# Start bytes in SBUF of the seven-product slabs: all their weights at byte 192 of 256, all their moving operands at byte 0

## The chip, the core and the metric

The kernel runs on one core of a Trainium2 chip. The metric is the device time of one execution in microseconds (us); the median of several executions stands for a kernel. A profile of one further execution gives each instruction's start on each engine. The two levels of TensorE's clock are 1.2 and 2.4 GHz; the profile gives the granted share of the full one. Throughout, "byte 192" is a start address in an SBUF partition modulo 256 bytes (64 float32 words, the constant `LINE`).

## What is computed

A forward pass over 512 tokens of width 1024, in float32: two gated feed-forward layers (width 2816) around a mixing layer with dilated attention and multi-scale pooling, then a retention layer and a stick-breaking attention layer. Cut to what the change touches:

```
def swiglu(x, w1, w3, w2):
    return (jax.nn.silu(x @ w1) * (x @ w3)) @ w2

h = h + 0.5 * swiglu(rms_norm(h, ffn1_norm[l]), ffn1_w1[l], ffn1_w3[l], ffn1_w2[l])
u = rms_norm(h, mix_norm[l])
proj = u @ w_in[l]                 # q, k, v, pooled part, two gates
...
merged = gates[:, :, 0] * y_attn + gates[:, :, 1] * y_pool
h = h + merged @ w_out[l]
h = h + 0.5 * swiglu(rms_norm(h, ffn2_norm[l]), ffn2_w1[l], ffn2_w3[l], ffn2_w2[l])
...
proj = u @ ret_w_in[i]             # q, k, v, g of the retention layer
```

## The kernel before

**Numbers.** Each float32 operand is split in a high and a low part (`w_hi` and `w_lo`, `x_hi` and `x_lo`), and a product is three matmuls: high weights by high x, high weights by low x, low weights by high x. These are the lines 2570 to 2572 (`passes`) and 2576 to 2578 (`joint`). In the trace's names the moving operand or the weights may come second: `acc<-x_hi,w_lo` has x moving and the low weights stationary, `acc<-w_hi,x_hi` has the slab moving and x stationary (value projections).

**Slabs.** Weights come in slabs of 2048 words a partition into `raw` (two slots, `RING`), by DMAs of the SP queue. ScalarE writes the high part (L736 for a plain slab), VectorE the low part (L1454), and TensorE works through them. TensorE may start on a slab when `w_ready` counts it; SP fetches the next into a slot when `w_ready` says that `raw` has been read. A plain slab is used in matmuls with 512 moving columns.

**Seven-product slabs.** Where a slab yields two independent 512x128 outputs from the same x, seven products of half size replace eight (Strassen's scheme). The program calls this `seven`. Each of the seven is 4 chunks of 3 matmuls, so 12 matmuls of 128x128 weights by 256 moving columns, 84 a slab. There are 57 such slabs in 8 stretches that follow on a plain slab: 7 and 11 in the first feed-forward layer, 2, 2 and 2 in the mixing layer, 8 and 11 in the second feed-forward layer, 14 in the retention layer (with four small transposes after the fourth of them, L2631). Four quarters of weights lie in the slab's slot (`s2`, `a11`, `s1`, `s3`), three in `wc_hi` and `wc_lo` (`a12`, `a22`, `s4`). The moving operands are quarters of `x_hi`/`x_lo` or the combinations `t1`, `t2`, `t3` in `xt_hi`/`xt_lo`.

The start bytes follow from the sizes of the tensors that are allocated ahead: `w_hi`, `w_lo`, `x_hi`, `x_lo` and `t4` start at byte 0, `xt_hi`, `xt_lo`, `wc_hi` and `wc_lo` at byte 192. A weight block is 512 bytes, a chunk of x 1024 or 2048, so all 12 matmuls of a product have the same two start bytes:

| product, in TensorE's order | weights | byte of weights, before | byte of moving operand, before | both after |
|---|---|---|---|---|
| 1 | a11 in w | 192 | 0 (x) | 192, 0 |
| 2 | s3 in w | 0 | 192 (t3 in xt) | 192, 0 |
| 3 | s2 in w | 0 | 192 (t2 in xt) | 192, 0 |
| 4 | a12 in wc | 192 | 0 (x) | 192, 0 |
| 5 | s1 in w | 0 | 192 (t1 in xt) | 192, 0 |
| 6 | a22 in wc | 192 | 0 (x or t4) | 192, 0 |
| 7 | s4 in wc | 192 | 0 (x) | 192, 0 |

Between products stand semaphore waits: ScalarE copies partial results out of PSUM (`snap`, L835; `snap_ready`) before products 3, 5 and 7 add to the same bank, and products 4 and 7 wait for the weights in `wc` (`wc_ready`). The order on every engine is written out by hand. ScalarE makes the slab's high parts in L780 (two quarters, `split_pair`) and L785 (the other two, `split_one`, which writes through the view `lone`), VectorE the low parts in L1556 and L1561. Ahead of the change `lone` spans two pieces, one at byte 0 and one at 192.

`first_col(k)` gives the column at which slab number k starts in its slot: 48 words (byte 192) for slabs of value projections, 0 for all others. Both the splitting (`prep`) and TensorE's `slab` use it, and `w_hi` and `w_lo` have 64 spare words a slot for it.

## Time and profile before

| | us |
|---|---|
| median of 3 executions | 1847.12 (1846.47 to 1848.96) |
| the profiled execution | 1845.56 |
| its span, first to last instruction | 1843.8 |
| TensorE busy in the span | 1828.2 (99%) |
| TensorE weight loads busy | 1636.9 (89%) |
| VectorE, ScalarE, GpSimd busy | 1396.5, 930.0, 81.5 |
| granted TensorE clock | 0.998 of full |

The profiled execution is 1.8 us from start to end longer than its span; what is taken off the span comes off it alike. It lies 1.6 us under the median. Matmuls overlap in the array and their ends are modelled, so what TensorE spends on a matmul is read from the distance of its start to the next start, and not from its duration.

### The profile page before, as it was taken

The page shows a single profiled execution, that of the slowest core. Times are in us where ns is not written, and L with a number is a line of the kernel's source. Part 1 is how long each engine was busy: PE and PEld are TensorE (multiplying, and loading weights), DVE is VectorE, ACT ScalarE, POOL GpSimd, SP SyncE. Part 2 cuts the span into 40 slices and gives each one's busy share as a digit, 9 for nine tenths or more (in the row PEclk, how much of TensorE's full clock was granted, in tenths as well). Part 3 has the DMA queues.
Part 4 walks back from the last instruction along what each step waited for, and adds up shares of the span by engine and source line. Part 5 has one row for each costly group of instructions (what it writes and reads, how often), then busy time and mean ns, then how long its engine had stood idle before and what let it go on. Part 6 is the DMA issues. An engine that isn't in the chain of part 4 may idle for free.

```text
span 1843.8 us, 28142 instructions
## 1 busy us (share of the span) xinstructions
PE 1828.2 (99%) x11305; PEld 1636.9 (89%) x11311; DVE 1396.5 (76%) x1912; ACT 930.0 (50%) x1274; POOL 81.5 (4%) x109
## 2 busy tenths in 40 slices
PE   9999999999999999999999999999999999999997
PEld 7998998888889988988998899988888888888886
DVE  8875887888778889866888987776777776666566
ACT  6652664435355536633653555455547644444445
POOL 0000000020001000000000000000000000000000
PEclk9999999999999999999999999999999999999999
DMA  6744763462407535743752678632231222222213
GB/s 215 181 120 133 199 161 116 164 158 77 114 26 210 155 114 149 188 149 110 191 146 95 199 211 240 231 137 77 107 137 61 79 92 69 92 81 79 91 68 92
DMA packets 60595, 244.78 MB, mean 133 GB/s; under 512 B 6865, under 2 KB 9457, under 8 KB 49857
## 3 DMA queue, kind: packets, MB, share of 16 engines
q1 hardware_dynamic: 46016, 199.25, 32.3%
q0 software_dynamic: 14032, 43.38, 12.3%
q8 instruction: 80, 1.31, 0.3%
q10 hardware_dynamic: 432, 0.56, 0.1%
q14 instruction: 35, 0.28, 0.0%
HBM read 223.76 MB, written 13.11 MB: 128 GB/s over the span
## 4 chain that ended last, share of the span: by engine, by line
PE 72%; DVE 5%; ACT 2%; issue 1%; DMA 0%; DVEq 0%; POOL 0%; ACTq 0%
PE acc L2570 14%; PE acc L2571 13%; PE acc L2572 13%; PE acc L2577 6%; PE acc L2576 6%; PE acc L2578 6%; PE att L2571 2%; PE att L2572 2%; PE att L2570 2%; PE att L2576 1%; PE att L2578 1%; PE att L2577 1%; DVE w_lo L1454 1%; PE acc L2838 1%; PE acc L2813 1%
## 5 line engine op out<-in xcount | busy, mean ns | idle before, releaser
L1454 DVE TENSOR_TENSOR w_lo<-raw,w_hi 128x2048 fp32r<-128x2048 f32 (+1 forms) x106 | 238.9, 2254 | 48.7 <-ACT w_hi L736 48.4
L736 ACT ACTIVATE w_hi<-raw 128x2048 fp32r<-128x2048 f32 (+1 forms) x106 | 199.3, 1880 | 75.3 <-PE acc L2572 61.9
L2570 PE MATMUL acc<-x_hi,w_hi 128*128 128x512 f32 x488 | 193.3, 396 | 0.9 <-DVE x_lo L1517 0.6
L2576 PE MATMUL acc<-xt_hi,w_hi 128*128 128x256 f32 x684 | 191.6, 280 | 0.0
L2578 PE MATMUL acc<-xt_hi,w_lo 128*128 128x256 f32 x684 | 191.3, 280 | 0.0
L2577 PE MATMUL acc<-xt_lo,w_hi 128*128 128x256 f32 x684 | 191.3, 280 | 0.0
L2572 PE MATMUL acc<-x_hi,w_lo 128*128 128x512 f32 x488 | 190.3, 390 | 0.0
L2571 PE MATMUL acc<-x_lo,w_hi 128*128 128x512 f32 x488 | 190.1, 390 | 0.0
L835 ACT ACTIVATE tmp<-acc 128x256 f32<-128x256 f32 x228 | 86.8, 380 | 124.6 <-PE acc L2578 114.8
L2571 PE MATMUL acc<-g_lo,w_hi 128*128 128x512 f32 x352 | 137.0, 389 | 0.0
L2570 PE MATMUL acc<-g_hi,w_hi 128*128 128x512 f32 x352 | 137.0, 389 | 0.0
L2572 PE MATMUL acc<-g_hi,w_lo 128*128 128x512 f32 x352 | 136.9, 389 | 0.0
L2576 PEld LDWEIGHTS acc<-xt_hi,w_hi 128*128 128x128 f32 x684 | 130.1, 190 | 0.1
L2578 PEld LDWEIGHTS acc<-xt_hi,w_lo 128*128 128x128 f32 x684 | 128.4, 188 | 0.0
L2577 PEld LDWEIGHTS acc<-xt_lo,w_hi 128*128 128x128 f32 x684 | 128.4, 188 | 0.0
L2570 PEld LDWEIGHTS acc<-x_hi,w_hi 128*128 128x128 f32 x488 | 91.6, 188 | 23.0 <-issue 2.7
L2576 PE MATMUL acc<-x_hi,wc_hi 128*128 128x256 f32 x400 | 110.5, 276 | 0.0
L2578 PE MATMUL acc<-x_hi,wc_lo 128*128 128x256 f32 x400 | 110.4, 276 | 0.0
L2577 PE MATMUL acc<-x_lo,wc_hi 128*128 128x256 f32 x400 | 110.4, 276 | 0.0
L2571 PEld LDWEIGHTS acc<-x_lo,w_hi 128*128 128x128 f32 x488 | 91.7, 188 | 20.1 <-issue 1.4
L2572 PEld LDWEIGHTS acc<-x_hi,w_lo 128*128 128x128 f32 x488 | 91.6, 188 | 19.2
L792 ACT ACTIVATE wc_hi<-raw_c 128x1024 fp32r<-128x1024 f32 x57 | 60.4, 1059 | 50.8 <-PE acc L2578 50.8
(510 smaller groups left out, 5116.0 us busy)
## 6 DMA issues: line engine op xcount, KB each, us to landing
raw<-in_ffn_down SPq DMA_DIRECT2D x32, 704.0 KB, 4.0
raw_c<-in_ffn_seven SPq DMA_DIRECT2D x37, 512.0 KB, 5.3
raw<-in_ffn_seven SPq DMA_DIRECT2D x33, 512.0 KB, 4.9
raw<-in_ffn_seven POOLq DMA_DIRECT2D x33, 512.0 KB, 7.4
raw<-in_ffn_seven SPq DMA_DIRECT2D x37, 256.0 KB, 4.6
raw<-in_ret_values SPq DMA_DIRECT2D x8, 1024.0 KB, 4.7
raw<-in_ret_out SPq DMA_DIRECT2D x8, 1024.0 KB, 6.8
raw<-in_sb_v SPq DMA_DIRECT2D x8, 1024.0 KB, 4.8
```

The costliest lines, as they stand in the source:

```text
L736: nc.scalar.activation(w_hi[:, slot, at:at + cols], raw[:, slot, 0:cols], ACT.Copy).then_inc(w_hi_ready, 1)
L792: nc.scalar.activation(wc_hi[:, cols], raw_c[:, third, :], ACT.Copy).then_inc(wc_hi_ready, 1)
L835: nc.scalar.activation(dst, src, ACT.Copy).then_inc(snap_ready, 1)
L1454: tt(w_lo[:, slot, at:at + cols], raw[:, slot, 0:cols], w_hi[:, slot, at:at + cols].bitcast(F32), ALU.subtract).then_inc(w_ready, 1)
L2570: mm(dst, still[0], move[0], start=first, stop=False)
L2571: mm(dst, still[0], move[1], start=False, stop=False)
L2572: return mm(dst, still[1], move[0], start=False, stop=last)
L2576: mm(dst, still[0], move[0], start=first, stop=False, skip_group_check=True)
L2577: mm(dst, still[0], move[1], start=False, stop=False, skip_group_check=True)
L2578: return mm(dst, still[1], move[0], start=False, stop=last, skip_group_check=True)
L2813: last = nc.tensor.transpose(dst[i // TB][:, P * (i % TB):P * (i % TB) + P], tmp[:, at:at + P], ident[:])
L2838: last = mm(dst, va[:, k_blk, value_slot(g, head)].rearrange("p s d -> p (s d)"), turned_probs[:, k % 2, i].rearrange("p s q -> p (s q)"), ...
```

## The change

No instruction is added, removed or put elsewhere: each engine has the same list in the same order. What differs is where operands lie.

- In a seven-product slab the four quarters lie one behind the other from byte 192 of the slot (`LATER_LINE`, 48 words). Before, they stood at words 0, 560, 1088 and 1600 of the slot: bytes 0, 192, 0 and 0. `lone` becomes one contiguous piece, `W_SUMMED` starts 16 words earlier.
- `xt_hi` and `xt_lo` move from byte 192 to byte 0, by padding ahead of them that is 48 words less, and 48 words more behind. `wc`, `x`, `t4` and all else stay.
- The plain slab ahead of each of the 8 stretches (`BEFORE_SEVEN`) starts at byte 192 instead of 0. These are 8 slabs with 318 matmuls of 512 columns in all: three of 48 (`x` by the last plain slab of the two feed-forward layers and the retention layer), two of 33 (the last down-projection slab of each first half) and three of 36 (the branch slabs of the mixing layer). Their moving operands are at byte 0.

```
--- before.py
+++ after.py
@@ -38,11 +38,12 @@
 MIX_SEVEN = DC - MIX_PLAIN
 QUART = SLAB // PARTS
 SUMMED = slice(2 * QUART, SLAB)
-W_SUMMED = slice(2 * QUART + 64, SLAB + 64)
 FILLED = {4: 2, 5: 2, 6: 1, 7: 2}
 PART = SLAB // PARTS
 RING = 2
 LINE = 64
+LATER_LINE = LINE * 3 // 4
+W_SUMMED = slice(LATER_LINE + 2 * QUART, LATER_LINE + SLAB)
 MIX_VALUES = 43, 44, 49
 SB_FIRST = 136
 BANKS = 4
@@ -196,7 +197,7 @@
 
         def lone(v, slot):
 
-            return v[:, slot, 0:2 * (QUART + LINE * 3 // 4)].rearrange("p (k q) -> p k q", k=2)[:, :, 0:QUART]
+            return v[:, slot, LATER_LINE:LATER_LINE + 2 * QUART].rearrange("p (k q) -> p k q", k=2)
 
         def pair_place(slot, ahead):
 
@@ -210,7 +211,7 @@
         def first_col(k):
 
             values = k in MIX_VALUES or k >= SB_FIRST and (k - SB_FIRST) % 4 == 0
-            return LINE * 3 // 4 if values else 0
+            return LATER_LINE if values or k in BEFORE_SEVEN else 0
 
         def half_row(c):
             return slice(TOK // 2 * (c % 2), TOK // 2 * (c % 2 + 1))
@@ -232,10 +233,10 @@
                 form_q = sb("form_q", [P, TB, TOK // 2], F32, under)
                 form_b = sb("form_b", [P, TB, TOK // 2], F32, under)
             g_lo = sb("g_lo", [P, HALF, TOK], F32R, scope)
-            sb("to_line_4", [P, 48 + 3 * DC * P], F32, scope)
+            sb("to_line_4", [P, 3 * DC * P], F32, scope)
             xt_hi = sb("xt_hi", [P, 3, TB, TOK // 2], F32R, scope)
             xt_lo = sb("xt_lo", [P, 3, TB, TOK // 2], F32R, scope)
-            sb("to_line_5", [P, 16], F32, scope)
+            sb("to_line_5", [P, LINE], F32, scope)
             raw_c = sb("raw_c", [P, RING, 2 * QUART], F32, scope)
             sb("to_line_6", [P, 48], F32, scope)
             wc_hi = sb("wc_hi", [P, 3 * QUART], F32R, scope)
@@ -453,6 +454,9 @@
         RET_FROM = sum(FFN_SEGS) + MIX_SEGS
         HEADS_FROM = RET_FROM + 2 * RET_PLAIN + PRODUCTS * RET_SEVEN
         UNIT_SLABS_FROM = 2 * (FC + 2 * DC) + MIX_SLABS
+        FFN_SLABS_FROM = 0, FC + 2 * DC + MIX_SLABS
+        BEFORE_SEVEN = ([FFN_SLABS_FROM[i] + FULL[i] - 1 for i in range(2)] + [FFN_SLABS_FROM[i] + HALF + DC - 1 for i in range(2)] +
+                        [FC + 2 * DC + BRANCH_FROM + 3 * j for j in range(1, DC // 2)] + [UNIT_SLABS_FROM + RET_PLAIN - 1])
         ACC_BEFORE_RET = 206
 
         def head_end(i, part):
@@ -2661,7 +2665,7 @@
                 slot = n.k % RING
                 n.next()
                 s2, a11, s1, s3 = ((w_hi[:, slot, at:at + QUART], w_lo[:, slot, at:at + QUART]) for at in
-                                   (0, QUART + LINE * 3 // 4, 2 * QUART + LINE, 3 * QUART + LINE))
+                                   (LATER_LINE + QUART * k for k in range(PARTS)))
                 a12, a22, s4 = ((wc_hi[:, QUART * k:QUART * (k + 1)], wc_lo[:, QUART * k:QUART * (k + 1)]) for k in range(3))
                 b11, b21, b22 = ((x_hi[:, rows, cols], x_lo[:, rows, cols]) for rows, cols in
                                  ((slice(0, TB), EARLY), (slice(TB, DC), EARLY), (slice(TB, DC), LATE)))
```

## Rows read from the trace of the kernel before

**Rows 1.** The page: busy time by engine, granted clock in 40 slices, chain by engine.

```profile
PE 1828.2 (99%) x11305; PEld 1636.9 (89%) x11311; DVE 1396.5 (76%) x1912; ACT 930.0 (50%) x1274; POOL 81.5 (4%) x109
...
PEclk9999999999999999999999999999999999999999
...
PE 72%; DVE 5%; ACT 2%; issue 1%; DMA 0%; DVEq 0%; POOL 0%; ACTq 0%
```

**Rows 2.** Timeline of TensorE, one seven-product slab: start us, modelled us, line, names.

```profile
219.89 0.28 PE L2576 MATMUL acc<-x_hi,w_hi 128*128 128x256 f32 x1
...
221.25 0.28 PE L2576 MATMUL acc<-xt_hi,w_hi 128*128 128x256 f32 x1
...
222.67 0.28 PE L2576 MATMUL acc<-xt_hi,w_hi 128*128 128x256 f32 x1
...
224.08 0.28 PE L2576 MATMUL att<-x_hi,wc_hi 128*128 128x256 f32 x1
...
225.50 0.28 PE L2576 MATMUL acc<-xt_hi,w_hi 128*128 128x256 f32 x1
...
226.87 0.28 PE L2576 MATMUL acc<-x_hi,wc_hi 128*128 128x256 f32 x1
...
228.23 0.28 PE L2576 MATMUL acc<-x_hi,wc_hi 128*128 128x256 f32 x1
...
229.59 0.28 PE L2576 MATMUL acc<-x_hi,w_hi 128*128 128x256 f32 x1
```

**Rows 3.** Line 2576 by names: count, modelled ns min/median/max, first and last start.

```profile
L2576 PE MATMUL acc<-xt_hi,w_hi x684: 276/281/387, 54.6 to 1183.8; 128*128 128x256 f32 x171
...
L2576 PE MATMUL att<-x_hi,wc_hi x228: 276/280/283, 57.5 to 1182.4; 128*128 128x256 f32 x114
```

**Rows 4.** Timeline of TensorE, first slab of a stretch: starts of products 1 and 2.

```profile
570.90 0.28 PE L2576 MATMUL acc<-x_hi,w_hi 128*128 128x256 f32 x1
...
572.31 0.28 PE L2576 MATMUL acc<-xt_hi,w_hi 128*128 128x256 f32 x1
```

**Rows 5.** Timeline of TensorE, last seven-product slab: products 3, 4, 5 and the end.

```profile
1179.71 0.28 PE L2578 MATMUL acc<-xt_hi,w_lo 128*128 128x256 f32 x1
1179.87 0.39 PE L2576 MATMUL acc<-xt_hi,w_hi 128*128 128x256 f32 x1
...
1181.35 0.28 PE L2576 MATMUL att<-x_hi,wc_hi 128*128 128x256 f32 x1
...
1182.71 0.28 PE L2576 MATMUL acc<-xt_hi,w_hi 128*128 128x256 f32 x1
...
1186.96 0.40 PE L2570 MATMUL acc<-w_hi,x_hi 128*128 128x512 f32 x1
```

**Rows 6.** Timeline of TensorE, the slab behind the four transposes of the retention stretch.

```profile
1089.31 0.60 PE L2631 MATMUL att<-ident,rstd 128*128 128x128 f32 x4
...
1089.98 0.28 PE L2578 MATMUL acc<-x_hi,w_lo 128*128 128x256 f32 x1
...
1091.11 0.28 PE L2576 MATMUL acc<-xt_hi,w_hi 128*128 128x256 f32 x1
```

**Rows 7.** Timeline of TensorE, value projection: first and last of 48 matmuls.

```profile
429.83 0.28 PE L2570 MATMUL acc<-w_hi,x_hi 128*128 128x256 f32 x1
...
435.37 0.28 PE L2572 MATMUL acc<-w_hi,x_lo 128*128 128x256 f32 x1
```

**Rows 8.** Timeline of TensorE, 264 matmuls of 512 columns between two stretches.

```profile
121.18 0.40 PE L2570 MATMUL acc<-g_hi,w_hi 128*128 128x512 f32 x1
...
181.04 0.28 PE L2576 MATMUL acc<-x_hi,w_hi 128*128 128x256 f32 x1
```

**Rows 9.** Windows: PE, PEld, DVE, ACT, POOL busy (count), clock, DMA share, GB/s.

```profile
210.20:219.90 9.70, 9.70 (x87) 9.70 (x86) 8.36 (x13) 6.17 (x10) 0.86 (x1) 1.00 0.74 196
```

**Rows 10.** Timeline of ScalarE in the slab of rows 2: the first snap.

```profile
221.45 0.38 ACT L835 ACTIVATE tmp<-acc 128x256 f32<-128x256 f32 x1
```

**Rows 11.** Lines by form: the split through `lone` on ScalarE, busy us, mean ns.

```profile
L785 ACT ACTIVATE w_hi<-raw 128x1024 fp32r<-128x1024 f32 x57 | 60.1, 1054 | 4.9 <-DVE raw L1543 4.9
```

More of the change, by code:

```diff
@@ L40 @@
 SUMMED = slice(2 * QUART, SLAB)
-W_SUMMED = slice(2 * QUART + 64, SLAB + 64)
 FILLED = {4: 2, 5: 2, 6: 1, 7: 2}
@@ L45 @@
 LINE = 64
+LATER_LINE = LINE * 3 // 4
+W_SUMMED = slice(LATER_LINE + 2 * QUART, LATER_LINE + SLAB)
 MIX_VALUES = 43, 44, 49
@@ L197, in lone @@
         def lone(v, slot):
-            return v[:, slot, 0:2 * (QUART + LINE * 3 // 4)].rearrange("p (k q) -> p k q", k=2)[:, :, 0:QUART]
+            return v[:, slot, LATER_LINE:LATER_LINE + 2 * QUART].rearrange("p (k q) -> p k q", k=2)
         def pair_place(slot, ahead):
@@ L212, in first_col @@
             values = k in MIX_VALUES or k >= SB_FIRST and (k - SB_FIRST) % 4 == 0
-            return LINE * 3 // 4 if values else 0
+            return LATER_LINE if values or k in BEFORE_SEVEN else 0
         def half_row(c):
@@ L234, in block_kernel @@
             g_lo = sb("g_lo", [P, HALF, TOK], F32R, scope)
-            sb("to_line_4", [P, 48 + 3 * DC * P], F32, scope)
+            sb("to_line_4", [P, 3 * DC * P], F32, scope)
             xt_hi = sb("xt_hi", [P, 3, TB, TOK // 2], F32R, scope)
             xt_lo = sb("xt_lo", [P, 3, TB, TOK // 2], F32R, scope)
-            sb("to_line_5", [P, 16], F32, scope)
+            sb("to_line_5", [P, LINE], F32, scope)
             raw_c = sb("raw_c", [P, RING, 2 * QUART], F32, scope)
@@ L455, in block_kernel @@
         UNIT_SLABS_FROM = 2 * (FC + 2 * DC) + MIX_SLABS
+        FFN_SLABS_FROM = 0, FC + 2 * DC + MIX_SLABS
+        BEFORE_SEVEN = ([FFN_SLABS_FROM[i] + FULL[i] - 1 for i in range(2)] + [FFN_SLABS_FROM[i] + HALF + DC - 1 for i in range(2)] +
+                        [FC + 2 * DC + BRANCH_FROM + 3 * j for j in range(1, DC // 2)] + [UNIT_SLABS_FROM + RET_PLAIN - 1])
         ACC_BEFORE_RET = 206
@@ L2663, in seven @@
                 s2, a11, s1, s3 = ((w_hi[:, slot, at:at + QUART], w_lo[:, slot, at:at + QUART]) for at in
-                                   (0, QUART + LINE * 3 // 4, 2 * QUART + LINE, 3 * QUART + LINE))
+                                   (LATER_LINE + QUART * k for k in range(PARTS)))
                 a12, a22, s4 = ((wc_hi[:, QUART * k:QUART * (k + 1)], wc_lo[:, QUART * k:QUART * (k + 1)]) for k in range(3))
```

## The prediction

> **What bounds the kernel now.** The page comes first. TensorE is busy 99% of the span at the full clock (2.4 GHz), and 72% of the chain that ended last is its own work, against 5% for VectorE and 2% for ScalarE [rows 1]. So time is won or lost where matmuls follow each other faster or slower, and a change of addresses can act there alone, unless another engine comes on top. The second view is the timeline of TensorE in one seven-product slab [rows 2]. Each product is 12 matmuls, so the distance of two starts over 12 is the pace of one matmul. Products 1, 6 and 7 take 1.36 us (113.3 ns a matmul), product 5 takes 1.37, products 2, 3 and 4 take 1.42, 1.41 and 1.42 (118 ns). The slab takes 9.70 us. The reader is to see two paces, 113.3 and about 117.9 ns, of instructions of one shape.
>
> The third view groups line 2576 by names [rows 3]. The modelled durations show the same two paces: the 684 matmuls with `xt` moving (products 2, 3 and 5) have a median of 281 ns and a minimum of 276, and product 4, whose operands lie at the same bytes as those of products 6 and 7, has 280 and 276. **The pair of start bytes alone does not set the pace.** Product 4 (192, 0) is slow and 6 and 7 (192, 0) are fast; products 2 and 3 (0, 192) are slow and 5 (0, 192) is fast. The pace behaves as a state that the stream carries along. I went through the boundaries of the 57 slabs for where it turns:
> - From (192, 0) to (0, 192), as from product 1 to 2 and 4 to 5, it turns: fast to slow, then slow to fast [rows 2].
> - From (0, 192) to (192, 0), as from 3 to 4 and 5 to 6, it stays what it was [rows 2].
> - Where the bytes stay the same (2 to 3, 6 to 7, and 7 to the next slab's 1) it stays too. In the last slab a stall of 0.16 us ahead of product 3 (1179.71 to 1179.87, 0.05 more than a step) turned the slow stream fast. Product 4 then took 1.36 us, and products 5 to 7 ran slow (4.25 us for 36 matmuls, 118 ns), over the boundary of 6 and 7 with its semaphore waits [rows 5]. So waits that are met early do not turn it, and a slow stream goes on at equal bytes.
> - Behind the plain slab, whose weights and x are both at byte 0, product 1 is slow: 1.41 us instead of 1.36, in 8 of 8 stretches [rows 4]. Behind the transposes it is fast (10 matmuls in 1.13 us) [rows 6].
>
> **The change part by part.** The order of all instructions stays, so each part is a price per matmul.
>
> *Seven-product slabs.* All 84 matmuls get (192, 0), the pair of the fast products 6, 7 and 1. No boundary within a stretch changes bytes any more. If the stream is fast, a slab takes 84 x 113.3 ns = 9.52 us instead of 9.70: 0.18 us less. 57 slabs give 10.3 us.
>
> *The entry.* 8 first slabs lose a slow product 1, 12 x 4.6 ns = 0.05 us each, 0.4 us. The last slab has 36 slow matmuls where others have none, and some fewer elsewhere; it gives about 0.05 us more. Sum: 10.7 us. Both the stall there and the one behind the transposes stay.
>
> *Whether the entry is fast.* This decides the sign, and the trace has no stream of 512 columns at (192, 0). Now the entry is a jump from (0, 0) to (192, 0), with 8 of 8 slow. With the plain slab at byte 192 as well there is no jump, only the change from 512 to 256 columns. All the turns in the steady slabs stand at boundaries where bytes change, so I take the entry as fast. But the rows do not exclude that the full 512-column stream ahead is itself what starts the slow pace: the value projection behind the pooling matmuls also starts slow out of 512-column matmuls, and keeps 117.9 ns for 47 steps (429.83 to 435.37) [rows 7].
>
> *The 8 plain slabs.* Their 318 matmuls of 512 columns run at 226.7 ns now: 264 of them take 59.86 us [rows 8]. At (192, 0) they could at worst pay the 4.6 ns that the slow 256-column matmul pays: 318 x 4.6 = 1.5 us. The start bytes have no visible price in the long streams, and a few steps where they change are under 0.03 us a slab. I take 0, nearest to rows 8, and keep 1.5 for the range; nothing below 0, since the mean there is exactly two fast steps of 256.
>
> *Other engines.* A seven-product slab costs VectorE 8.36 and ScalarE 6.17 of its 9.70 us [rows 9]. At 9.52 they still fit, with 1.1 us left on VectorE. The tightest wait is that on `snap`: it starts at 221.45, lasts 0.38, and TensorE wants it for product 3 at 222.67, 0.84 us later [rows 2, 10]. Product 2, which covers it, gets only 0.06 us shorter. If the cover were gone, each stall would be paid in full, as the one in rows 5. `lone` in one piece is the same 1024 words, 1054 ns on ScalarE [rows 11]; it is off TensorE's path, cost 0. The DMA share of 0.74 rises to about 0.75. All this goes at nothing.
>
> Against the profiled execution: 1845.56 - 10.7 = 1834.9 us, and since what changes is inside the span, the median goes from 1847.12 to **1836.4 us**, 0.58% less.
>
> **The rivals.**
> - *Slow throughout.* If 512 columns into 256 starts slow whatever the bytes, nothing turns the stream back before its end: today the turn from product 4 to 5 does that in every slab, and the change removes it. A slow slab takes 84 x 117.9 = 9.90 us, 0.20 more than now. That holds for the 47 slabs ahead of the transposes and elsewhere; the 10 behind them start fast [rows 6] and gain 0.18. 47 x 0.20 - 10 x 0.18 = +7.6 us: 1854.7 us. It decides in the first matmuls of each stretch; for it speak rows 7 and the persistence in rows 5, against it that every turn in steady slabs comes with a change of bytes. If the 10 also fell slow, it were +11.4 us, 1858.5.
> - *Some stretches.* Entries could differ: the mixing layer's come out of branch slabs with `o_hi` moving, others out of `x` or `g`. Or a slow entry heals after some slabs. Half the slabs fast and half slow is about zero, three quarters fast gives -10.3 x 0.75 + 57 x 0.25 x 0.20 = -4.9 us. So 1839 to 1847, centre 1842. For it: the entries are 8 separate events. Against it: all 8 are alike now.
> - *It does nothing.* The pace may come from what is read against what in time, not from start bytes, with the turns made by something else that stands at the same products; then 1847.1 us. For it: one pair of bytes has both paces [rows 2]. Against it: the turns repeat in each slab at the same boundaries. The Trainium skill is on this rival's side: the page "SBUF — State Buffer", section "Who interferes with whom", says that TensorE has two independent read ports, one for the moving operand and one for the weights, and waits on nobody. By that rule no address would matter, and the trace does not agree as far as the pace goes: equal shapes at 113.3 and 118 ns.
>
> **How the numbers follow.** Fast throughout: 0.58, at 1836.4 us, of its own range 1835 to 1838.5 (the 1.5 us of the plain slabs, and 0.5 either way for the executions). Some stretches: 0.12. Nothing: 0.10. Slow: 0.20. The predicted time is that of the first. The range must leave out no more than 0.2: it runs from 1834.5 to 1850.0, over the first three cases and up to what a partly slow kernel gives, and leaves out the slow one. A measurement of this kernel tells about 0.2% (3.7 us) from no change, so faster is below 1843.4 and slower above 1850.8. Faster takes the 0.58 and 0.09 of the mixed case, 0.67; same takes 0.03 of that and the 0.10, 0.13; slower 0.20.
>
> **What would show it.** In the changed kernel's timeline the starts of all seven products of a slab should be 1.36 us apart and a slab 9.52; the group with `xt` moving should have a median of 276 ns like the others, and the group into `att` too. Product 1 of a stretch's first slab shows the entry: 1.36 us for fast, 1.41 for slow, and in the latter case the whole stretch should show 1.41 until its end, except behind the transposes. The plain slabs at byte 192 should keep 227 ns. Snap ends should lie over 0.7 us ahead of product 3, and VectorE's sum in a slab should stay near 8.4 us. The prediction is wrong if entries are slow, if fast streams turn slow at equal bytes, or if the 512-column matmuls at (192, 0) run slower.

## The result

The changed kernel took **1856.99 us** (median of 5 runs, 1855.19 to 1857.53) where the kernel before, run beside it, took 1846.74 (5 runs, 1846.34 to 1848.96): a ratio of 1.0053, with an interval of 1.0042 to 1.0065. It is 0.53% slower. The prediction had been 1836.4 us with a range up to 1850.0, so sign and range are both wrong. The time is nearest to that of the rival "slow throughout" in its harder form, 1858.5 us, in which the ten slabs behind the transposes are slow too; it lies 1.5 us below it.

The page of the changed kernel (span 1855.2 us, 1843.8 before) shows where the time is. First the busy time by engine and the clock, then the chain by engine:

```profile
PE 1840.1 (99%) x11305; PEld 1648.6 (89%) x11311; DVE 1396.8 (75%) x1912; ACT 931.8 (50%) x1274; POOL 81.5 (4%) x109
...
PEclk9999999999999999999999999999999999999999
...
PE 94%; DVE 3%; ACT 1%; issue 1%; DMA 0%; DVEq 0%; ACTq 0%; POOL 0%
```

Against [rows 1] the counts of instructions are the same and the clock is the same. VectorE and ScalarE grew by 0.3 and 1.8 us, TensorE by 11.9, and the chain went from 72% TensorE to 94%. So the added time is TensorE's own. Where it is, the timeline shows for the slab that answers to [rows 2]. The columns are start, modelled us, line and names; the lines of the changed kernel are four higher:

```profile
212.26 0.28 PE L2580 MATMUL acc<-x_hi,w_hi 128*128 128x256 f32 x1
...
213.67 0.28 PE L2580 MATMUL acc<-xt_hi,w_hi 128*128 128x256 f32 x1
...
216.50 0.28 PE L2580 MATMUL att<-x_hi,wc_hi 128*128 128x256 f32 x1
217.91 0.28 PE L2580 MATMUL acc<-xt_hi,w_hi 128*128 128x256 f32 x1
219.33 0.28 PE L2580 MATMUL acc<-x_hi,wc_hi 128*128 128x256 f32 x1
...
222.15 0.28 PE L2580 MATMUL acc<-x_hi,w_hi 128*128 128x256 f32 x1
```

Product 1 takes 1.41 us (213.67 - 212.26), products 2 and 3 together 2.83, product 4 1.41, product 5 1.42, products 6 and 7 together 2.82. The slab takes 9.89 us: 84 matmuls at 117.8 ns. The two paces inside a slab are gone, as forecast, but what is left is the slow one.

Two groups of the view by names answer to [rows 3] (count, modelled ns min/median/max, first and last start):

```profile
L2580 PE MATMUL acc<-xt_hi,w_hi x684: 279/279/279, 54.8 to 1195.2; 128*128 128x256 f32 x171
...
L2580 PE MATMUL att<-x_hi,wc_hi x228: 279/279/279, 57.6 to 1193.8; 128*128 128x256 f32 x114
```

Minimum, median and maximum are one number. Before, the minimum was 276, the mark of the fast pace. All 57 slabs run slow from the first to the last, without one exception. They take 564.00 us in sum, 553.65 before: **10.35 of the 11.4 us**. The rest is in two places. The 318 matmuls of 512 columns in the plain slabs now follow each other at 226, 229 and 232 ns in turn, 228.8 on average instead of 226.7 [rows 8], which is 0.7 us. And 96 matmuls of 256 columns of the value projection at 410.9 us, which the diff does not touch, run at 117.8 ns instead of 113.3, 0.4 us. (In both traces that projection begins behind a stall of 0.14 to 0.16 us, out of which it came fast in the one and slow in the other.)

### The profile page after: what moved, and what is told of

Read it like the earlier page. It is cut to its first block, busy times and chain, and to the rows that moved or that the text cites. A ratio compares the mean times of both kernels' runs of the same rounds, so it can differ in the third digit from the quotient of the medians.

```text
span 1855.2 us, 28142 instructions
## 1 busy us (share of the span) xinstructions
PE 1840.1 (99%) x11305; PEld 1648.6 (89%) x11311; DVE 1396.8 (75%) x1912; ACT 931.8 (50%) x1274; POOL 81.5 (4%) x109
## 4 chain that ended last, share of the span: by engine, by line
PE 94%; DVE 3%; ACT 1%; issue 1%; DMA 0%; DVEq 0%; ACTq 0%; POOL 0%
PE acc L2574 17%; PE acc L2575 17%; PE acc L2576 17%; PE acc L2582 9%; PE acc L2581 9%; PE acc L2580 9%; PE att L2575 2%; PE att L2576 2%; PE att L2574 2%; PE att L2582 1%; PE att L2581 1%; PE att L2580 1%; PE acc L2842 1%; PE acc L2817 1%; DVE w_lo L1458 0%
```

## The experiments

A pair like (192, 0) is the start byte of the weights and of the moving columns. "Slow" and "fast" are the paces of 117.8 and 113.3 ns a matmul of 256 columns, 9.893 and 9.520 us a slab. The 512-column matmuls of a plain slab have their own, longer steps. A step is the distance of one matmul's start to the next start; "entered behind a 226" says that the step from the last 512-column matmul to the first 256-column one of a stretch was 226 ns. Most kernels below were run once, and are judged by the steps and slabs in their trace and not by their time; where a ratio with an interval stands, there were several runs. Two theories stand against each other at the start: that the entry from the plain slabs starts the slow pace and nothing turns it back, and that the bytes themselves have a price.

**Each half alone.** The first kernel takes only the plain slabs back, the second is the kernel before with only the plain slabs moved.

```
 # e1_sevens_only, against the changed kernel
-            return LATER_LINE if values or k in BEFORE_SEVEN else 0
+            return LATER_LINE if values else 0
 # e2_plain_only, against the kernel before
-            return LINE * 3 // 4 if values else 0
+            return LINE * 3 // 4 if values or k in BEFORE_SEVEN else 0
```

> The change without its last part: the plain slab ahead of each stretch stays at byte 0, the seven-product slabs are all at (192, 0). Theory H (the pace is carried along: the stretch keeps the pace with which it is entered, and out of 512-column matmuls that pace is slow): all 57 slabs slow at 9.89 us as in the changed kernel, the 318 matmuls of the plain slabs back at 226.7 ns instead of 228.8, so about 1856.3 us, 0.7 under the changed kernel. Rival P (the plain slab at byte 192 is what makes the entry slow): product 1 fast at 1.36 us and slabs of 9.52 us, about 1836 us.

> The kernel before with the plain slab ahead of each stretch at byte 192 and nothing else. Theory H: product 1 of each stretch stays slow at 1.41 us, the later slabs stay at 9.70 us with products 2, 3 and 4 slow, and the 318 matmuls of 512 columns cost 2.1 ns more each, 0.7 us: 1847.8 us. Rival P: product 1 takes another pace than 1.41 us, and products 5 to 7 may turn slow, over 1850 us.

Sevens only: 1856.17 us against 1846.63, ratio 1.0050 (1.0033 to 1.0066), all 57 slabs slow. Plain slabs only: 1847.75 against 1846.63, ratio 1.0003 (0.9994 to 1.0013), slabs of 9.70 us as before. The loss is that of the sevens. The plain slabs' new byte, which was to make the entry fast, made it fast in two of eight stretches: the second and third mixing stretch of this kernel begin with a product 1 of 1.36 us (first slab 9.700 us, 9.748 in the other unstalled ones), against theory H's "stays slow". The other six were entered behind a 226, these two behind a 232. In the kernel with only the sevens changed all eight are slow, behind a 225 or 226. The difference of the two kinds of entry comes back below.

**Other bytes for the weights.** `SEVEN_AT` stands in the place of 48 words in the sevens and in the plain slabs ahead of them: 16 words (byte 64), then 32 (byte 128).

```
+SEVEN_AT = 16
+W_SUMMED = slice(SEVEN_AT + 2 * QUART, SEVEN_AT + SLAB)
...
+            return LATER_LINE if values else SEVEN_AT if k in BEFORE_SEVEN else 0
```

> The changed kernel with all seven-product weights (w and wc) and the 8 plain slabs at byte 64 instead of 192, moving operands at byte 0. Theory H (any equal pair keeps the pace of the entry): slabs of 9.89 us, 1857 us. Rival D (each difference of start bytes has a pace of its own, and that of 192 and 0 is a slow one): another pace, at best 9.52 us a slab and 1836 us, at worst the 120 ns that matmuls at equal bytes show elsewhere, 10.1 us a slab and 1868 us.

> As with byte 64, now byte 128 for all seven-product weights and the 8 plain slabs. Theory H: slabs of 9.89 us, 1857 us. Rival D: another pace, between 9.52 us a slab (1836 us) and 10.1 us a slab (1868 us).

At byte 128 every slab takes 9.96 to 9.98 us (two with a stall more), 1862.83 us in all, and the steps wander between 112 and 125 ns instead of keeping to one pace: those bytes do have a price of their own. At byte 64 (1850.86 us, span 1849.1) something new appears. The 22 slabs of the two stretches behind the down projection run fast from their first product, the 35 of the other six are slow, at the same bytes and with the same code. So at byte 64 the bytes alone do not set the pace; it differs from stretch to stretch, by how a stretch is entered or by what it is.

**Byte 64 with other plain slabs.** Only the plain slabs' byte differs from the run at 64: `0` or `LATER_LINE` in place of `SEVEN_AT` in the last line above.

> Seven-product weights at byte 64 as in the run before, where the two stretches of 11 behind the down-projection ran fast (9.52 us a slab) and the six others slow (9.89), but the 8 plain slabs ahead stay at byte 0. Theory H (the entry decides, and the pace is then carried on at equal bytes): the entries from byte 0 make some stretches fast or slow as a whole; from (0, 0) the entry to (192, 0) was always slow, so all slow, 1856 us. Rival C (what made two entries fast is the down-projection's own count or operands, not its byte): the same two stretches stay fast, about 1848.5 us.

> Seven-product weights at byte 64, the 8 plain slabs ahead at byte 192. Theory H: each stretch is fast or slow as a whole by its entry; nothing says which, between 1836 and 1857 us. Rival C: again the two stretches of 11 fast and the others slow, about 1849 us. A pace that changes within a stretch at equal bytes speaks against H.

With plain slabs at 0 all 57 slabs are slow (1856.85 us, span 1855.1). With plain slabs at 192 (1855.21, span 1853.4) the first mixing stretch had a stall of 0.4 us ahead of product 5 and one of 0.1 us behind its first matmul, ran fast from the fifth matmul of product 5 on, and the next two mixing stretches were then entered fast, behind a 233; all others were slow, behind a 225 or 226. Rival C falls in both kernels. The pace did change within a stretch at equal bytes, which had been named as a sign against H, but it did so at a stall: a short stall can turn the pace, and the next stretch, behind a slab of 512-column matmuls, was then fast too.

**One product with other bytes.** In the changed kernel without its plain slabs' move, product 5 alone gets its old pair (0, 192), by its own place for `s1` and `t1`:

```
-                                   (LATER_LINE + QUART * k for k in range(PARTS)))
+                                   (2 * QUART + LATER_LINE, 3 * QUART + LATER_LINE, 0, QUART + LATER_LINE))
...
+XT_AT = LATER_LINE, LINE + TB_COLS, LINE + 2 * TB_COLS
...
```

> All seven products at (192, 0) but the fifth, whose weights stay at byte 0 and whose moving combination t1 stays at byte 192; plain slabs at byte 0. Theory T (the jump from (192, 0) to (0, 192) turns the pace, the way back does not): the pace turns once a slab, so slabs alternate: one with products 1 to 4 slow and 5 to 7 fast, the next with 1 to 4 fast and 5 to 7 slow, about 9.71 us on average, about 1847 us. Rival A (a uniform (192, 0) falls back to slow by itself, and fast needs a jump in each slab): products 5 to 7 fast and 1 to 4 slow in every slab or all slow, 1848 to 1856 us.

1848.86 us, span 1847.1. The timeline of two neighbouring slabs, first matmuls of their products:

```profile
196.04 0.28 PE L2594 MATMUL att<-x_hi,wc_hi 128*128 128x256 f32 x1
...
197.46 0.28 PE L2594 MATMUL acc<-xt_hi,w_hi 128*128 128x256 f32 x1
...
198.83 0.28 PE L2594 MATMUL acc<-x_hi,wc_hi 128*128 128x256 f32 x1
...
201.55 0.28 PE L2594 MATMUL acc<-x_hi,w_hi 128*128 128x256 f32 x1
...
205.63 0.28 PE L2594 MATMUL att<-x_hi,wc_hi 128*128 128x256 f32 x1
...
206.99 0.28 PE L2594 MATMUL acc<-xt_hi,w_hi 128*128 128x256 f32 x1
...
208.41 0.28 PE L2594 MATMUL acc<-x_hi,wc_hi 128*128 128x256 f32 x1
```

Product 4 takes 1.42 us (slow), product 5 1.37, products 6 and 7 2.72 together (fast). The next slab is still fast in product 4 (1.36) and slow from product 5 on (1.42). Each slab's one change to (0, 192) turns the pace and it is carried on over the slab's boundary, so that slabs alternate between 9.745 and 9.688 us. In the first slab of seven stretches the change turns nothing (9.896 us, slow throughout); in that of the first mixing stretch a stall ahead of product 5 comes on top, and it is fast behind it.

**Turning it with idle matmuls.** These kernels are built on the one with only the sevens changed (sevens at 192, plain slabs at 0, all slow). Ahead of product 4, or of products 2 and 4, of each stretch's first slab they issue idle matmuls with the pair (0, 192), whose result the product overwrites. Shown is the version with four at each of two places; in the others the number is 1 or 12, or only the second place is used:

```
+            def turn(dst, behind):
...
+                if behind in BEFORE_SEVEN:
+                    for _ in range(4):
+                        mm(dst, x_hi[:, TB + 1, 0:P], x_hi[:, TB + 1, 48:48 + TOK // 2], start=True, stop=True, skip_group_check=True)
...
+                turn(one[:, EARLY], n.k - 2)
                 product(one[:, EARLY], s3, t3, True)
...
+                turn(aside, n.k - 2)
+                product(aside, a12, b21, True)
```

> Sevens all at (192, 0), plain slabs at byte 0, and in the first slab of each stretch four idle matmuls of 256 columns ahead of product 4, with weights at byte 0 and moving operand at byte 192, whose result product 4 overwrites. Theory T (one such jump turns the pace, and equal bytes then keep it): products 1 to 3 of the first slab slow, all behind it fast, slabs of 9.52 us, about 1840 us. Rival A (a uniform (192, 0) is slow by itself): back to slow behind the four, about 1860 us.

> The sevens as in the changed kernel, the plain slabs back at byte 0 (the run with only the sevens changed: profiled span 1854.7 us, all 57 seven slabs slow, 9.893 us). In the first seven slab of each of the eight stretches, four idle matmuls with weights at byte 0 and moving columns at byte 192 stand ahead of product 2 and four more ahead of product 4; their result is overwritten by the product behind them. Theory A (the pace of a stretch is a state that equal bytes carry on; behind 512-column matmuls the first change of bytes doesn't turn it, the second does): in a first slab products 1 to 3 stay at 117.8 ns a matmul, products 4 to 7 run at 113.3, and all 49 slabs behind the first ones take 9.52 us. Slabs: 49 x 0.37 = 18.3 us less; first slabs 8 x 48 x 4.5 ns = 1.7 less, and 8 x 8 idle matmuls x 0.118 = 7.6 more: span near 1842.3, the time near 1844. Theory B (what turned the pace in the kernel before is not the change of bytes itself but something that idle matmuls lack, such as the products' own length, so they turn nothing, as four ahead of product 4 turned nothing): all slabs stay at 9.893, span 1854.7 + 7.6 = 1862.3.

> As the kernel with four idle matmuls ahead of products 2 and 4 of each first slab, but with one at each place instead of four. Theory A: if one matmul at other bytes is a change of bytes as good as four, the pace turns from product 4 on and the slabs behind take 9.52 us; cost 8 x 2 x 0.118 = 1.9 us, gain 18.3 + 1.7: span near 1836.6, the time near 1839, a ratio to the kernel before of 0.996. If the turn needs more than one matmul at the other bytes: all slow, 1854.7 + 1.9 = 1856.6. Theory B says that too: 1856.6.

> As the kernel with four idle matmuls at weights 0 and moving 192 ahead of products 2 and 4 of each first slab (all slow, 1861.9 us), with twelve at each place, as many as a product has. If a stay at other bytes must be as long as a product's to turn the pace, a first slab runs fast from product 4 on and the 49 slabs behind take 9.520 us: 1854.7 + 8 x 24 x 0.118 - 49 x 0.373 - 1.7 = 1857.4. If idle matmuls that read one place again and again don't turn it whatever their number, all stay slow: 1854.7 + 22.7 = 1877.4.

One group of four: all slow, 1860.45 us. Two groups of four: all slow, 1863.65 us, with a span of 1861.9 where the rival, that idle matmuls turn nothing, had said 1862.3. Two groups of one: all slow, 1858.31 us against 1846.12, ratio 1.0066 (1.0049 to 1.0083). After these the theory that a change of bytes turns the pace looked fallen. The last run, with twelve at each place, brought it back. The timeline of its stretch at 182.9 us, first matmuls of products and the groups of idle ones (line 2666):

```profile
182.86 0.28 PE L2580 MATMUL acc<-x_hi,w_hi 128*128 128x256 f32 x1
...
184.27 1.58 PE L2666 MATMUL acc<-x_hi 128*128 128x256 f32 x12
...
185.68 0.28 PE L2580 MATMUL acc<-xt_hi,w_hi 128*128 128x256 f32 x1
...
188.51 1.53 PE L2666 MATMUL att<-x_hi 128*128 128x256 f32 x12
...
189.88 0.28 PE L2580 MATMUL att<-x_hi,wc_hi 128*128 128x256 f32 x1
...
191.25 0.28 PE L2580 MATMUL acc<-xt_hi,w_hi 128*128 128x256 f32 x1
```

Behind the first group product 2 is slow (with product 3, 2.83 us for 24). The second group itself takes 1.37 us and what follows is fast: product 4 1.37, and the slab behind 9.520. That is so in all eight stretches. So the second change of bytes turns a slow stream when the stay at the other bytes is twelve matmuls long, and not when it is four. Of the 49 slabs behind first slabs 42 were entered fast, at the changed kernel's own bytes. The span is 1861.5 against 1857.4 expected: the last slabs of the four longer stretches ahead of the retention layer take 9.84 (1.3 us more), since a stall ahead of product 5 (steps of 167 and 224 to 228 ns) turns them slow, and a like stall between products 4 and 5 of the third slab behind the transposes (slab 49, counted from 0) turned it and the seven behind it slow (3.0 us more).

**Counting the matmuls in front.** In the run at byte 64 the 512-column matmuls of the plain slabs follow each other at 231 and 236 ns in turn. The eight entries, with the last three steps of 512 columns and the first three of 256, worked out from the starts in the trace's records, in the run at 64 and in the one with matmuls added that follows:

```
byte 64, none added                   byte 64, one added in six
 start  last 512     first 256         start  last 512     first 256
  53.3  232 236 230  119 116 119        53.9  236 231 236  118 113 114
 182.6  236 232 236  117 114 114       180.8  236 230 236  119 113 113  none added
 571.0  231 235 231  119 117 117       569.3  236 231 236  118 114 113
 599.1  231 235 231  119 117 117       597.6  233 233 234  121 116 114
 627.3  232 235 230  120 117 117       625.2  230 236 231  118 118 117
 724.6  231 237 231  117 119 117       722.7  235 231 236  118 114 113
 863.8  235 231 236  118 114 112       859.1  236 231 235  119 113 113  none added
1052.4  231 236 231  117 119 117      1048.0  236 231 236  118 114 113
```

Without one added, the two fast stretches (182.6 and 863.8) are entered behind a 236, the six slow stretches behind a 230 or 231. So the first matmul of the plain slab is issued once more, in the six slow cases, and in a second kernel in all eight:

```
+            again = set(set(BEFORE_SEVEN) - {FFN_SLABS_FROM[i] + HALF + DC - 1 for i in range(2)})
...
             def passes(dst, still, move, first, last):
...
+                if first and n.k - 1 in again:
+                    again.remove(n.k - 1)
+                    mm(dst, still[0], move[0], start=True, stop=True)
```

> Base: the kernel with the weights of sevens and of the plain slabs in front of them at byte 64 (one look: 1850.86 us, profiled span 1849.1; the 22 slabs of the two stretches behind the down projection run 9.520 us, the 35 of the six other stretches 9.893). In its plain slabs the 512-column matmuls follow each other at 231 and 236 ns in turn; the two fast stretches were entered on a 236, the six slow ones on a 230 or 231. Here the first matmul of the plain slab in front of each of the six slow stretches is issued twice (once more 128x512, overwritten by the second), and nothing else is changed. Theory P (the pace at the entry is the phase in which the stream of matmuls stands to the reads of SBUF, and the parity of the matmuls at byte 64 sets it): all eight stretches are entered on a 236 and all 57 slabs run 9.52 us; 35 x 0.373 = 13.1 us less, 6 x 0.233 = 1.4 more, span near 1837.4, the time near 1839.2, a ratio to the kernel before of 0.996. Theory Q (the pace at the entry hangs on what the stretch or its slab is, not on the count): the same two stretches are fast, span 1849.1 + 1.4 = 1850.5.

> As the kernel with one more matmul in six of the plain slabs, but with one in all eight, so also in front of the two stretches that were fast before. Theory P: the count's parity turns there too, so that these two are entered on a 231 and their 22 slabs go to 9.893 while the 35 others go to 9.520: span 1849.1 - 13.1 + 22 x 0.373 + 8 x 0.233 = 1846.1. Theory Q: as before, 22 fast and 35 slow, 1849.1 + 1.9 = 1851.0.

Here one matmul alone changes the pace. The entry of the first stretch, byte 64 without the added matmul, then with it:

```profile
52.83 0.40 PE L2576 MATMUL acc<-x_lo,w_hi 128*128 128x512 f32 x1
53.07 0.39 PE L2577 MATMUL acc<-x_hi,w_lo 128*128 128x512 f32 x1
53.30 0.28 PE L2581 MATMUL acc<-x_hi,w_hi 128*128 128x256 f32 x1
53.42 0.28 PE L2582 MATMUL acc<-x_lo,w_hi 128*128 128x256 f32 x1
53.53 0.28 PE L2583 MATMUL acc<-x_hi,w_lo 128*128 128x256 f32 x1
53.65 0.28 PE L2581 MATMUL acc<-x_hi,w_hi 128*128 128x256 f32 x1
```

```profile
53.47 0.39 PE L2581 MATMUL acc<-x_lo,w_hi 128*128 128x512 f32 x1
53.70 0.40 PE L2582 MATMUL acc<-x_hi,w_lo 128*128 128x512 f32 x1
53.94 0.28 PE L2586 MATMUL acc<-x_hi,w_hi 128*128 128x256 f32 x1
54.06 0.28 PE L2587 MATMUL acc<-x_lo,w_hi 128*128 128x256 f32 x1
54.17 0.28 PE L2588 MATMUL acc<-x_hi,w_lo 128*128 128x256 f32 x1
54.28 0.28 PE L2586 MATMUL acc<-x_hi,w_hi 128*128 128x256 f32 x1
```

The last 512-column matmul is modelled at 0.39 us and followed by a step of 0.23 in the one, and modelled at 0.40 with a step of 0.24 in the other, and the fourth start comes 0.35 and 0.34 us behind the first. That is how small the sign is; what it tells lasts for seven slabs, 9.893 us each against 9.520 (9.693 in the last, which has a stall). With one added in six, five of these six stretches and the two others are entered fast: 1843.73 us against 1846.30, ratio 0.9985 (0.9975 to 0.9994), span 1840.7. The sixth, the third mixing stretch, was slow. With one in all eight (1849.01 us, span 1847.2), the two stretches behind the down projection became slow, all 22 slabs at 9.893, and the five stretches other than the second mixing one fast. Theory Q, that the pace hangs on the stretch, falls. One entry in the table stands outside the pattern: the second mixing stretch (597.6) was fast out of even steps of 233 ns, with no long and short ones in turn. For the six a span of 1837.4 was expected and 1840.7 came, 3.3 us more. Some 2.3 us are two stretches that turned slow midway. The first of these turns comes with a stall of 0.04 us:

```profile
574.65 0.28 PE L2588 MATMUL att<-x_hi,wc_lo 128*128 128x256 f32 x1
574.76 0.32 PE L2586 MATMUL acc<-xt_hi,w_hi 128*128 128x256 f32 x1
574.91 0.28 PE L2587 MATMUL acc<-xt_lo,w_hi 128*128 128x256 f32 x1
575.03 0.28 PE L2588 MATMUL acc<-xt_hi,w_lo 128*128 128x256 f32 x1
```

The matmul that opens product 5 holds 0.04 us longer than its neighbours (0.32), the next starts 0.15 us behind it instead of 0.11, and what follows is slow to the end of the stretch. (The program has a semaphore wait ahead of this product; the view of waits lists none on TensorE here, so that the stall is a wait is taken from its place.) Slab 52 has a like stall at product 5 (0.08 us), and the four behind it are slow. The last slabs of two more stretches have a stall (0.35 us together). The rest, 0.75 us, is the third mixing stretch, slow from its entry: with a matmul added, each had the opposite pace of the one before it; without one, in the run at 64, the same.

**The same count at the change's own bytes.** In the changed kernel the steps in front go 226, 229, 232, and all eight stretches are entered behind a 226. One or two matmuls more move that:

```
+            more = {k: 2 for k in BEFORE_SEVEN}
...
             def passes(dst, still, move, first, last):
...
+                if first:
+                    for _ in range(more.pop(n.k - 1, 0)):
+                        mm(dst, still[0], move[0], start=True, stop=True)
```

> The changed kernel (weights of sevens and plain slabs at byte 192, x at 0; span 1855.2 us, all 57 seven slabs at 9.893) with the first 512-column matmul of each of the eight plain slabs issued three times instead of once, nothing else. In these slabs of the changed kernel the matmuls follow each other at 226, 229 and 232 ns in turn, and all eight stretches are entered behind a 226. With the plain slabs at 192 and the sevens at 64 two stretches were fast, both entered behind a 233. Theory P (a phase that each matmul moves on, and where the last 512-column one leaves it sets the pace of all that follows): two more move each entry on by two, to behind a 232 or 233, and all 57 slabs run 9.520 us: 57 x 0.373 = 21.3 less, 16 x 0.229 = 3.7 more, span near 1837.6. Theory Q (the cycle belongs to the operands, which come in threes, and repeating one moves nothing; the pace at these bytes is the slow one): 1855.2 + 3.7 = 1858.9.

> As the changed kernel with two more matmuls in each plain slab, but with one more. Theory P: the entries come behind a 229; whether that phase is a fast or a slow one no run has shown. The fast one is one of three here, so slow is the likelier: span 1855.2 + 8 x 0.229 = 1857.0; were it fast, 1855.2 - 21.3 + 1.8 = 1835.7. Theory Q: 1857.0, with the entries behind a 226 as in the changed kernel.

With two more, six of the eight stretches are entered behind a 231 or 232 and are fast from the first step; the second mixing one is entered behind a 229 and the third behind a 226, both slow. With one more, seven are entered behind a 229 or 230 and one behind a 226, all slow, 1859.41 us. The two kernels differ from the changed one by 16 and 8 matmuls and from each other by 8:

```
first stretch          last 512      first 256         pace
changed kernel         229 232 226   117 119 117       117.8
one more               231 226 229   120 118 117       117.8
two more               226 229 232   113 113 114       113.3
```

So the entry at (192, 0) is slow in the changed kernel because of where in the cycle it happens to fall. With two more the time was 1847.07 us, the span 1845.3 and not 1837.6. The 4 slabs of the two mixing stretches are slow (1.5 us), and so are those behind the transposes, which turned the stream here (3.4 for nine); stalls in the last two slabs cost 1.3, and the last slabs of the four longer stretches take 9.84 us (1.3).

**No cycle, no count.** With the plain slabs at byte 0 the steps are an even 226.7 ns; one matmul more in front of four stretches, two in front of the others:

```
+            more = {k: 1 + i % 2 for i, k in enumerate(sorted(BEFORE_SEVEN))}
```

> The kernel with only the sevens changed (plain slabs at byte 0, all 57 seven slabs at 9.893 us, span 1854.7) with one more 512-column matmul in front of the first, third, fifth and seventh stretch and two more in front of the others; nothing else. At byte 0 the 512-column matmuls follow each other at an even 226.7 ns, so that there is no cycle that a count could move. Theory P in its narrow form (only matmuls that go in a cycle have a phase to hand on): every stretch is entered behind a 226 and stays slow, span 1854.7 + 12 x 0.227 = 1857.4. Theory P in its wide form (a count moves the phase at any bytes): the stretches with one or those with two more turn fast, some 9 to 12 us less: 1845 to 1849.

1861.37 us, every slab slow and every entry behind a 225 or 226: there is nothing that a count could move. The span is 2.2 us above the expected 1857.4, by waits in the first mixing slab and in the last two slabs. Nine kernels here, the one before among them, have their plain slabs at byte 0, and all 72 entries are slow, as the 8 of 8 of the kernel before [rows 4]. Whether the even steps or the jump of bytes does it there is not separated, since each of the nine has both. Elsewhere the jump does not decide: the changed kernel has none and is slow, and with the plain slabs at 192 and the sevens at 64 two entries over a jump are fast.

**A version that beats both.** Byte 64, one matmul added in four plain slabs, none in front of the second and third mixing stretch:

```
...
+            more = {k: 1 for k in BEFORE_SEVEN[:2] + BEFORE_SEVEN[4:5] + BEFORE_SEVEN[-1:]}
```

> The kernel with the weights of sevens and plain slabs at byte 64 and one more matmul in six of the eight plain slabs had three slow pieces left: the slab behind a short wait in the first mixing stretch and its neighbour, the third mixing stretch, and five slabs at the end behind another short wait. Here the second and third mixing stretch get no additional matmul, since from one mixing stretch to the next a fast one without an additional matmul should stay fast; four are added in all. Theory P: all eight stretches are entered on a 236; with no wait in a stretch all 57 slabs run 9.520, span 1837.0; each wait of a stretch can turn the rest of it, at 0.37 us a slab: 1837.0 to 1840.5, the time 1838.5 to 1843. Theory Q: the two stretches without an additional matmul are slow as in the kernel with none, 1.5 us more than that.

**1842.39 us** (10 runs, 1839.23 to 1842.89) against 1846.28 (13 runs): ratio 0.9975, interval 0.9966 to 0.9985. It is 0.25% faster than the kernel before. In the profiled execution (span 1838.1) all 57 slabs are fast, 544.44 us in sum, 1.8 above 57 x 9.52 by stalls. The group with `xt` moving, to be set beside [rows 3]:

```profile
L2586 PE MATMUL acc<-xt_hi,w_hi x684: 276/276/387, 55.0 to 1178.0; 128*128 128x256 f32 x171
```

Three of its ten runs took 1839.2 to 1839.9 us, seven 1842.3 to 1842.9. One profile shows one of the first kind; that in the others a stall turned some eight slabs slow (8 x 0.37 = 3.0 us) is argued from the other traces, not shown. A stall does not turn the stream always: in this profile one at product 5 of slab 18 cost 0.46 us, and the fast pace went on behind it.

```profile
574.74 0.28 PE L2588 MATMUL att<-x_hi,wc_lo 128*128 128x256 f32 x1
575.20 0.39 PE L2586 MATMUL acc<-xt_hi,w_hi 128*128 128x256 f32 x1 [0.18 <-ACT tmp L840]
575.42 0.28 PE L2587 MATMUL acc<-xt_lo,w_hi 128*128 128x256 f32 x1
```

The last slabs of the long stretches show more of this. A fast stream meets a like stall there at product 5. With the weights at byte 64 (steps of 164 to 169 and 221 to 223 ns) it stayed fast in 12 of 12 cases, in four kernels (slab 9.69 us). With the weights at 192 (166 to 168 and 224 to 228 ns) it came out slow in 8 of 8 (9.84 us), in the kernel with two more matmuls and the one with twelve idle ones. So byte 64 holds the fast pace better over this stall. Why is not shown.

## Why the prediction was wrong

- **What bounds the kernel** was right: all of the difference is TensorE's own pace, at the same count of instructions and the same clock. That the pace is a state which the stream carries along was right too, and each later run leans on it.
- **"Whether the entry is fast"** is the step that failed. It took the entry as fast because in the steady slabs all turns stand where bytes change, and so gave 0.58 to the fast case. The trace of before had two signs against it, and the text named both: 8 of 8 entries slow [rows 4], and a slow value projection behind 512-column matmuls [rows 7]. It read the first as a jump of bytes that the change would remove. The runs show that the pace follows the last step of the 512-column stream (at unchanged bytes slow behind a 226 or 229, fast behind a 232), and that equal bytes give no claim to the fast one. A third sign was not named: the prediction says that the change from (192, 0) to (0, 192) turns the pace, but in the eight first slabs of before product 2 is slow behind a slow product 1 (both 1.41 us), so that there the change of bytes turned nothing. And the slow case lost more than the entry: in the kernel before, the change at product 5 brought each slab back to the fast pace, as the run with product 5 alone and the one with twelve idle matmuls show; the rival said this, the main case did not need it.
- **Seven-product slabs.** The sizes were right to 0.01 us: 9.52 for a fast slab, in every run that had some, and 9.893 for a slow one where the rival had 9.90. Only the state was the other one: +10.35 us in place of -10.3.
- **The 10 slabs behind the transposes** were taken to start fast whatever came before [rows 6]. They start slow in the changed kernel, though product 1 has the same bytes as before:

```profile
1099.04 0.60 PE L2635 MATMUL att<-ident,rstd 128*128 128x128 f32 x4
1099.40 0.36 PE L2580 MATMUL acc<-x_hi,w_hi 128*128 128x256 f32 x1
...
1099.72 0.28 PE L2582 MATMUL acc<-x_hi,w_lo 128*128 128x256 f32 x1
...
1100.90 0.28 PE L2580 MATMUL acc<-xt_hi,w_hi 128*128 128x256 f32 x1
```

  From the third matmul to product 2 it is 1.18 us, 1.13 before. In [rows 6] the slab ahead had ended fast, here it ended slow. In 17 of the 18 kernels that have the two paces (all but the one at byte 128) the pace behind the transposes is that ahead of them; the kernel with two more matmuls went over them from fast to slow. Taking them as fast made the rival's first price, 1854.7, too small by 3.8 us.
- **The 8 plain slabs** were taken at 0 with a bound of 1.5 us; they cost 0.7 (318 x 2.1 ns). The term was mis-sized, inside its bound.
- **Other engines** at nothing was right; in the best version, where a slab takes 9.52 us, VectorE still fits with 8.3 of 9.6:

```profile
209.00:218.60 9.60, 9.60 (x87) 9.60 (x86) 8.33 (x13) 6.21 (x11) 0.86 (x1) 1.00 0.73 211
```

- **The range** ended at 1850.0 and left out the case that came, to which the text gave 0.20. The text itself said that the rows do not exclude a slow entry [rows 7]; with 8 slow entries of 8 and one persistent slow stream on record, 0.20 looks low in hindsight.
- **The page that was weighed.** The Trainium skill's rule ("SBUF — State Buffer", "Who interferes with whom": two independent read ports, TensorE waits on nobody) made the rival of no change. The section speaks of who waits for whose port and does not name start bytes; read as "no address matters", as the prediction read it, it does not agree with the runs: slabs with one list of matmuls and one clock take 9.520, 9.893 or 9.97 us by where the operands lie and how the stream was entered.

What stays open: what in TensorE or SBUF the state is; why twelve matmuls at other bytes turn it and four do not (nothing between was run); why the first change of bytes behind a slow 512-column entry turns nothing and the second does; whether a slow entry out of byte 0 comes from the even steps or from the jump of bytes; why a mixing stretch with a matmul added takes the other pace than the one before it; and which stalls turn the stream.

## What to carry to other kernels

When a trace shows two paces for instructions of one shape and one pair of addresses, ask first how the stream enters and what turns it, before asking which addresses are good: removing every change of bytes also removed what brought a slow stream back in each slab. Look at the steps between starts in nanoseconds at the last matmuls ahead of a long stream; where they go in a cycle (231 and 236, or 226, 229 and 232), one or two additional matmuls at 0.23 us each can be worth 0.37 us for each slab that follows. Such a gain is fragile, since a stall of 0.04 us can turn the stream back, so measure it in ten runs and not in one.

## What the runs showed of the hardware

- A stream of 128x256 matmuls at full clock has two stable paces at one pair of addresses, 113.3 and 117.8 ns (9.520 and 9.893 us for 84), and keeps either for 100 us (the slow one in each stretch of 11 slabs of the changed kernel, 108.8 us; the fast one for 100.6 us in the last kernel, until a stall). A fast mixing stretch followed on a fast mixing stretch over 36 matmuls of 512 columns where no matmul was added, and the pace went over four transposes in 17 of 18 kernels.
- Where a slow stream went for twelve 256-column matmuls to other start bytes (weights 0, moving 192) and back, the second such visit of a stretch turned it fast in 8 of 8 stretches; two visits of four, or of one, turned it in none.
- 512-column matmuls take 226.7 ns with the weights at byte 0, 228.8 at 192 (226, 229, 232 in turn) and 233.3 at 64 (231 and 236 in turn, in one plain slab an even 233), the moving columns at byte 0.
- With the weights at byte 128 a slab without a longer stall took 118.5 to 118.8 ns a matmul, with single steps of 112 to 125, and never ran at 113.3 throughout.
- Nine kernels had plain slabs at byte 64 or 192 (sevens at 64, at 192 or as before): of their 72 stretches the 31 entered behind the longest step of the cycle (231 to 233 ns at 192, 235 to 236 at 64) were fast from the start, 40 entered behind another step were slow, and one out of even steps of 233 was fast. With plain slabs at byte 0 (even 226.7) all 72 were slow.
- A like short stall (0.16 us in two steps) left a fast stream fast in 12 of 12 cases with the weights at byte 64 and turned it slow in 8 of 8 at 192.
